# A two-layer decoder kernel on one core: forget rows from sigmoids, and the recurrent value projection by seven half-size products

## What is computed

```python
def hgrn2_mixer(u, w_in, lb, out_gain, w_out):
    q, fl, inp, g = split(u @ w_in)             # each 512 x 1024, 8 heads of 128
    log_f = logaddexp(log(lb), log1p(-lb) + log_sigmoid(fl))
    k = -expm1(log_f)
    # per head: b = cumsum(log_f); scores_ts = sum_d q_td k_sd exp(b_td - b_sd), s <= t
    # o = scores @ inp + (q exp(b)) @ state; o = rms_norm(o) * out_gain * silu(g)
    return o @ w_out
```

## Time and profile before

| | us |
|---|---|
| median of 3 runs (lowest, highest) | 2130.0 (2129.38, 2132.3) |
| the profiled execution, its time | 2130.18 |
| its span in the trace | 2126.7 |

### The profile page before, as it was taken

One profiled execution on the slowest core, in us unless ns is written; L12 is line 12 of the kernel. 1 busy time (PEld: TensorE's weight loads), 2 busy tenths in 40 slices (PEclk: granted clock), 3 DMA queues, 4 the chain that ended last, 5 costly groups with the idle time before them and its releaser, 6 DMA issues.

```text
span 2126.7 us, 20583 instructions
## 1 busy us (share of the span) xinstructions
PE 1986.8 (93%) x8264; PEld 1002.0 (47%) x8264; DVE 631.7 (30%) x1413; ACT 421.8 (20%) x833; POOL 268.4 (13%) x367
## 2 busy tenths in 40 slices
PE   8999999999999999999996998989898899979896
PEld 4588854444555544545543533424343434324333
DVE  2355542212888423242535101002020202001012
ACT  1033331116666211102311000100000010100002
POOL 3433100002767200001110000000000000000000
PEclk9999999999999999999998999999999999999998
DMA  9022230202110502411333699999999999999995
GB/s 265 3 60 60 91 138 0 80 10 88 60 40 25 212 16 99 121 40 40 109 130 158 272 427 428 427 427 427 427 428 428 427 427 427 427 428 425 428 425 201
DMA packets 100141, 486.59 MB, mean 229 GB/s; under 512 B 5855, under 2 KB 50234, under 8 KB 75984
## 3 DMA queue, kind: packets, MB, share of 16 engines
q1 hardware_dynamic: 97376, 480.79, 56.2%
q0 software_dynamic: 2384, 4.39, 0.7%
q10 hardware_dynamic: 288, 0.11, 0.0%
HBM read 483.13 MB, written 2.34 MB: 228 GB/s over the span
## 4 chain that ended last, share of the span: by engine, by line
PE 78%; DMA 12%; DVE 7%; ACT 2%; issue 1%; POOL 0%; POOLq 0%; ACTq 0%; DVEq 0%
PE bank L888 17%; PE bank L1370 13%; DMA arena<-in_w_up 12%; PE bank L1401 10%; PE bank L880 10%; PE bank L961 6%; PE bank L1321 3%; PE bank L1239 3%; PE bank L1347 2%; PE bank L985 2%; PE bank L1391 2%; PE bank L1125 1%; DVE arena L2033 1%; DVE arena L2032 1%; PE bank L870 1%
## 5 line engine op out<-in xcount | busy, mean ns | idle before, releaser
L1370 PE MATMUL bank<-arena 128*64 128x512 f32 x2048 | 466.3, 613 | 70.7 <-DMA arena<-in_w_up 70.6
L888 PE MATMUL bank<-arena 128*128 128x512 f32 x832 | 361.9, 595 | 5.1 <-issue 4.2
L1370 PEld LDWEIGHTS bank<-arena 128*64 128x64 f32 x2048 | 160.3, 141 | 373.7 <-issue 373.5
L880 PE MATMUL bank<-arena 128*128 128x512 f32 x672 | 295.3, 597 | 0.3
L888 PEld LDWEIGHTS bank<-arena 128*128 128x128 f32 x832 | 157.4, 191 | 198.8 <-issue 197.6
L1401 PE MATMUL bank<-arena 128*64 128x512 f32 x960 | 219.8, 617 | 0.0
L880 PEld LDWEIGHTS bank<-arena 128*128 128x128 f32 x672 | 127.2, 192 | 155.3 <-issue 155.1
L1456 ACT ACTIVATE arena<-bank 128x512 f32<-128x512 f32 (+3 forms) x134 | 72.7, 548 | 474.5 <-PE bank L888 193.2
L2382 DVE TENSOR_TENSOR arena<-arena,bank 128x512 f32<-128x512 f32 x64 | 42.0, 684 | 409.7 <-PE bank L1347 409.1
L2397 DVE TENSOR_TENSOR arena<-bank,arena 64x512 f32<-64x512 f32 x64 | 44.5, 695 | 365.5 <-ACT arena L1708 363.9
L1708 ACT ACTIVATE arena<-bank 64x512 f32<-64x512 f32 x64 | 37.6, 588 | 552.6 <-PE bank L1370 510.6
(11 more groups left out here) (308 smaller groups left out, 1800.0 us busy)
## 6 DMA issues: line engine op xcount, KB each, us to landing
arena<-in_w_gate SPq DMA_DIRECT2D x64, 2048.0 KB, 24.1
arena<-in_w_up SPq DMA_DIRECT2D x64, 2048.0 KB, 28.2
arena<-in_w_down SPq DMA_DIRECT2D x60, 2048.0 KB, 23.9
arena<-in_att_w_in SPq DMA_DIRECT2D x24, 512.0 KB, 7.3
arena<-in_rec_w_in SPq DMA_DIRECT2D x12, 1024.0 KB, 5.7
arena<-in_ple_w_gate SPq DMA_DIRECT2D x4, 2048.0 KB, 11.8
arena<-in_w_down SPq DMA_DIRECT2D x8, 1024.0 KB, 15.3
arena<-in_w_in SPq DMA_DIRECT2D x6, 1024.0 KB, 8.3
```

The lines of the kernel that those rows point to most:

```text
L880: mm = pe.matmul(bank[:, :], w[:, k, c:c + P], xT[:, k, :], start=(k == 0), stop=(k == KT - 1))
L888: mm = pe.matmul(bank[:, 0:n], xT[:, k, P * i:P * i + P], w[:, k, c:c + n], start=(k == 0), stop=(k == kt - 1))
L1370: mm = pe.matmul(banks[f][64 * part:64 * part + 64, :], xe[:, k, CAP * (e % 2):CAP * (e % 2) + CAP], w[:, kk, 512 * f:512 * f + 512], star ...
```

## The change

1. `i1` by seven products instead of eight (Strassen's scheme in Winograd's form). The 512 tokens are split into tiles (0, 1) and (2, 3), the 1024 channels and the 1024 columns into halves. Each of products 1 to 7 is done for two tiles, 4 matmuls of 512 columns each (`row_product`): 14 jobs, 56 matmuls. VectorE makes four sums of weights (`i1_weight_sum`, 128 x 2048 each, between the steps of `tail(0)`; the fourth goes to a buffer of its own), eight sums of tokens (128 x 512) after tile 3 is turned, and 14 additions of results, of which ScalarE did none before. ScalarE reverses tile 1 whole and half of tile 3, and drains four jobs instead of eight.
2. The forget rows from sigmoid(f) and sigmoid(-f), read straight from the bank; k and its reversed part by a scaled copy; log_f by one ln with scale and bias. VectorE keeps only the running sum.
3. In the head loop VectorE takes `forget_sum(h+2)` and levels 0 to 3 of `exponents(h+2)` ahead of the states of head h, level 4 before the mean, levels 5 and 6 after it. ScalarE takes `forget_rows(h+2)` ahead of the copy of the turned k, and `level_exps(h+2)` right after `chunk_exps(h+1)`. At the head start it copies both q rows before `level_exps(0)`.
4. Waits and loads named after `("i1", 3, 1)` are named after `("i1", 7, 1)`, the new last job.

```diff
+    def row_ending():
+        yield ("i1", 1, 0), "act"
+        yield from pre(1, 2)
+        yield ("i1", 1, 1), "act"
+        yield from row_part("i1", 2)
+        yield from pre(1, 3)
+        for p in (4, 6, 5, 3, 7):
+            yield from row_part("i1", p)
...
-        rec_slab("f1", 1, 4096, ("i1", 3, 1))
-        rec_slab("g1", 0, 6144, ("i1", 3, 1))
+        rec_slab("f1", 1, 4096, ("i1", 7, 1))
+        rec_slab("g1", 0, 6144, ("i1", 7, 1))
...
+            def row_product(name, x, w):
+                bank = job_bank(name)
+                for k in range(4):
+                    mm = pe.matmul(bank[:, :], x[:, k, :], w[:, k, :], start=(k == 0), stop=(k == 3))
+                mm.then_inc(filled, 1)
...
+            def input_rows():
+                wlo, whi = need_slab(pe, ("i1", 0)), need_slab(pe, ("i1", 1))
+                (s1, s2, s3, s4), (t1, t2, t4) = i1_sums, i1_weights
+                tile_done(("u", 1), 0)
+                row_product(("i1", 1, 0), UT[:, 0:4, 0:P], wlo[:, 0:4, :])
+                pre(1, 2, u_rows[0])
+                pe.wait_ge(tile_reversed, 1)
+                row_product(("i1", 1, 1), tile_1r[:, 0:4, :], wlo[:, 0:4, :])
+                row_product(("i1", 2, 0), UT[:, 4:8, 0:P], wlo[:, 4:8, :])
+                row_product(("i1", 2, 1), tile_1r[:, 4:8, :], wlo[:, 4:8, :])
+                pre(1, 3, u_rows[1])
+                pe.wait_ge(i1_summed, 4)
+                tile_done(("u", 1), 2)
+                row_product(("i1", 4, 0), UT[:, 4:8, 2 * P:3 * P], t4)
+                pe.wait_ge(tile_reversed, 2)
+                row_product(("i1", 4, 1), tile_3r, t4)
+                tile_done(("u", 1), 3)
+                for p, ready, x, w in ((6, 8, s2, t2), (5, 8, s1, t1), (3, 10, s4, whi[:, 4:8, :]), (7, 12, s3, whi[:, 0:4, :])):
+                    pe.wait_ge(i1_summed, ready)
+                    for t in range(2):
+                        row_product(("i1", p, t), x[:, :, P * t:P * t + P], w)
...
             def forget_in(h):
-                w = fwork[h % 2]
                 if h >= 2:
-                    act.wait_ge(f_dve, 3 * (h - 2) + 2)
+                    act.wait_ge(f_dve, h - 1)
+                if h >= 1:
+                    act.wait_ge(f_act, 2 * (h - 1) + 1)
                 act.wait_ge(filled, nth(("f1", h)))
                 bank = led.bank(("f1", h))
-                act.activation(w[0], bank[:, :], ACT.Identity)
-                act.activation(w[1], bank[:, :], ACT.Abs).then_inc(by_act, 1)
...
+                act.activation(logf1[h % 2], bank[:, :], ACT.Sigmoid)
+                act.activation(other1, bank[:, :], ACT.Sigmoid, scale=-1.0).then_inc(by_act, 1)
+
+            def forget_rows(h):
+                if h >= 2:
+                    act.wait_ge(filled, nth(("diag", h - 2)))
+                    act.wait_ge(decayed, 16 * (h - 2) + 16)
                 act.wait_ge(*drained(("f1", h)))
...
+                act.wait_ge(lb_dve, 2)
+                rest = lw[2][:, h:h + 1]
+                act.activation(k1[h % 2], other1, ACT.Identity, scale=rest)
+                act.activation(k1r[h % 2], other1.rearrange("p (c t) -> p c t", c=TT)[:, 1::2, ::-1], ACT.Identity, scale=rest
                                ).then_inc(f_act, 1)
...
+                act.activation(logf1[h % 2], logf1[h % 2], ACT.Ln, bias=lw[3][:, h:h + 1], scale=rest).then_inc(f_act, 1)
...
-            forget_in(0)
-            forget_softplus(0)
-            forget_in(1)
-            forget_floor(0)
-            copy(q1[0], ("q1", 0))
+            for h in range(2):
+                forget_in(h)
+                forget_rows(h)
+            for h in range(2):
+                copy(q1[h], ("q1", h))
             level_exps(0)
             chunk_exps(0)
...
+            level_exps(1)
             for h in range(RH):
-                if h + 1 < RH:
-                    level_exps(h + 1)
+                if h + 2 < RH:
+                    forget_rows(h + 2)
                 copy(kw1[:, :, :], ("kw", h), src=lambda b: b[:, 0:384].rearrange("p (c t) -> p c t", c=3))
...
                 if h + 1 < RH:
                     chunk_exps(h + 1)
+                if h + 2 < RH:
+                    level_exps(h + 2)
...
                 ple(2)
                 transposed(("h", layer), 3, 1, hT2, None)
                 turned(1)
+                if layer == 0:
+                    i1_weight_sum(1)
                 rows(2)
                 ple(3)
                 rows(3)
+                if layer == 0:
+                    i1_weight_sum(2)
                 turned(2)
+                if layer == 0:
+                    i1_weight_sum(3)
+                    i1_early_rows()
                 turned(3)
...
                 if h + 2 < RH:
-                    forget_log(h + 2)
+                    forget_sum(h + 2)
+                    exponents(h + 2, range(4))
                 head_states(h)
                 if h + 1 < RH:
                     chunk_exponents(h + 1)
...
                 if h + 2 < RH:
-                    forget_sum(h + 2)
+                    exponents(h + 2, range(4, 5))
                 head_mean_square(h)
                 if h + 2 < RH:
-                    exponents(h + 2)
+                    exponents(h + 2, range(5, LEVELS))
```

More of the change, by code:

```diff
@@ L179, in tail @@
                 yield from middle
+        if layer == 0:
+            yield from row_ending()
+            return
         yield from follow(0)
@@ L216, in psum_jobs @@
                 yield from joint("g0", m // 2)
-    yield from tail(0, lambda i: rows(("i1", i), "act", "act"))
+    yield from tail(0, None)
     for tag, h in FIRST_HEADS:
@@ L927, in tail @@
                         middle()
+                if layer == 0:
+                    follow()
+                    return
                 for i in range(TT):
@@ L1554, in _ @@
-            act.wait_ge(lb_dve, 2)
-            act.activation(lw[2], lw[1], ACT.Exp).then_inc(lb_act, 1)
-            act.wait_ge(lb_act, 1)
-            act.activation(lw[2], lw[2], ACT.Ln, bias=1.0).then_inc(lb_act, 1)
+            act.wait_ge(*drained(("u", 1, 1, 1)))
+            act.wait_ge(filled, nth(("gate", 0, 3, 1)))
+            act.activation(tile_1r, UT[:, :, P:2 * P][:, :, ::-1], ACT.Identity).then_inc(tile_reversed, 1)
+            for t in range(2):
+                copy(i1_first[t], ("i1", 1, t))
@@ L1559, in forget_in @@
+            act.wait_ge(*drained(("u", 1, 3, 1)))
+            act.activation(tile_3r, UT[:, 4:8, 3 * P:4 * P][:, :, ::-1], ACT.Identity).then_inc(tile_reversed, 1)
+            for t in range(2):
+                copy(i1[:, 2 + t, 0:512], ("i1", 4, t))
+            act.wait_ge(lb_dve, 1)
+            act.activation(lw[1], lw[0], ACT.Sigmoid).then_inc(lb_act, 1)
+            act.activation(lw[2], lw[0], ACT.Sigmoid, scale=-1.0).then_inc(lb_act, 1)
             def forget_in(h):
-                w = fwork[h % 2]
@@ new lines, in i1_early_rows, with i1_rows, block, token_sum @@
+            def i1_early_rows():
+                for t in range(2):
+                    dve.wait_ge(*drained(("i1", 1, t)))
+                    dve.wait_ge(filled, nth(("i1", 2, t)))
+                    dve.tensor_tensor(i1[:, t, 0:512], led.bank(("i1", 2, t))[:, :], i1_first[t], ALU.add).then_inc(by_dve, 1)
+            def i1_rows():
+                s1, s2, s3, s4 = i1_sums
+                def block(k, late, t):
+                    x = UT[:, 4 * k:4 * k + 4, P * (2 * late + t):P * (2 * late + t) + P]
+                    return x[:, :, ::-1] if t else x
+                def token_sum(dst, t, one, two, op):
+                    dve.tensor_tensor(dst[:, :, P * t:P * t + P], one, two, op).then_inc(i1_summed, 1)
+                def part(x, t):
+                    return x[:, :, P * t:P * t + P]
+                dve.wait_ge(*drained(("u", 1, 3, 1)))
+                for t in range(2):
+                    token_sum(s1, t, block(0, 1, t), block(1, 1, t), ALU.add)
+                for t in range(2):
+                    dve.wait_ge(i1_summed, 5 + t)
+                    token_sum(s2, t, part(s1, t), block(0, 0, t), ALU.subtract)
+                for t in range(2):
+                    dve.wait_ge(i1_summed, 7 + t)
+                    token_sum(s4, t, block(1, 0, t), part(s2, t), ALU.subtract)
+                for t in range(2):
+                    token_sum(s3, t, block(0, 0, t), block(0, 1, t), ALU.subtract)
+                def add(dst, p, t, more):
+                    dve.wait_ge(filled, nth(("i1", p, t)))
+                    return dve.tensor_tensor(dst, led.bank(("i1", p, t))[:, :], more, ALU.add)
+                lo, hi = slice(0, 512), slice(512, 1024)
+                first, second, fourth = i1_first, i1_second, i1_fourth
+                for t in range(2):
+                    add(second[t], 6, t, first[t]).then_inc(by_dve, 1)
+                for t in range(2):
+                    dve.wait_ge(*drained(("i1", 6, t)))
+                    dve.wait_ge(*drained(("i1", 4, t)))
```

(11 more changed lines are left out.)

118 lines of the change are left out of this document (45 added, 73 removed).

## The result

| | us |
|---|---|
| changed kernel, median of 4 runs (lowest, highest) | 2113.2 (2111.6, 2118.2) |
| kernel before, median of 4 runs beside it (lowest, highest) | 2130.6 (2129.4, 2132.3) |
| ratio of the two, with its 95% interval | 0.9913 [0.9894, 0.9931] |
| profiled execution of after: span | 2110.3 |

What follows compares the result with a forecast made beforehand. TensorE's matmuls were taken to bound the `i1` stage and, at 21.6 us per head plus waits and slow clock, the head loop. 2130.2 - 6.7 (products) - 16.6 (loop) = 2106.9, forecast 2107, range 2104.5 to 2114.

Steps and rivals of the forecast that it cites:

- A head therefore costs TensorE 21.6: Head loop: TensorE needs 21.6 us per head, so the other engines may save only its waits and the slow clock.
- Products, -6.7: Stage of `i1`: 16 fewer instructions save 6.87 us, less a wait of 0.15; the projections start at 480.5.
- Head start, 0: Start of the heads: `level_exps(0)` comes 2 us later behind both q copies, within five us of room, so no change.
- Loop, -16.6: Head loop: waits -13.6, slow clock -4.0, a new wait in head 0 +1.0; bounds -17.6 and -13.8.
- The slack of 2.3: Head loop: room of 2.3 us between VectorE's eight rows ending at 10.6 and its state copies from 12.9.
- VectorE near 17 a head: Head loop: VectorE loses four groups of instructions, 3.6 of 20.5 us per head, leaving 16.9.
- The norm: Head loop: VectorE's norm ends 21 us after the diagonal job, slack 4 before the next head's sixth level job.
- Clock: Head loop: slow stretches in three heads, 4.0 us together, go with the waits; clock 1.00.
- rival 1: Head loop: VectorE late at the states in every head; about 2122, by half of that 2113; chance 0.13.
- rival 4: Head loop: VectorE and GpSimd slow each other, slower than before; 2155 if all rows take 1.48; chance 0.04.
- Rivals 3 and 5: Products in `i1` don't pay, 2114, chance 0.06; sigmoids need as many table loads on ScalarE, 2108, within the forecast.
- rival 2: Head loop: waits gone but slow clock stays, following short waits too; 2111; chance 0.06.

Runs made afterwards that it cites:

- early exponentials: Changed kernel with level_exps(1) right behind chunk_exps(0), ahead of the gate copies: 2109.8 us in one execution, 2110.1 when timed.
- ln first: Changed kernel with level_exps(1) right behind chunk_exps(0) and, in the forget rows, the ln ahead of the two scaled copies for k: 2106.4 us.
- products alone: Kernel before with the seven products only, forget rows and both lists of the head loop as before: 2123.7 us, ratio 0.996.
- VectorE's old list: Changed kernel with ScalarE's new list kept, but VectorE's head-loop list in the order of before: 2137.9 us, ratio 1.0028.
- GpSimd nearly still: Changed kernel with GpSimd's level multiplies of heads 1 to 7 on one column, values of those heads left out: 2098.7 us in one execution.
- both old lists: Changed kernel with VectorE's and ScalarE's head-loop lists in the order of before, sigmoid rows and products kept: 2121.1 us, ratio 0.9948.
- six rows: Changed kernel with level_exps(1) right behind chunk_exps(0) and six exponent rows ahead of the states instead of eight: 2111.2 us, ratio 0.9902.

## Why the prediction was right, and where not

The time fell in the range, with help from its width. The forecast loop was 7.6 us too short, which by itself puts the sum at 2114.5, above the range; 0.7 less in the other stages and 2.4 us around the span instead of 3.5 brought it to 2112.7. And by its own signs the account failed: TensorE waits for the copies of the states in every head from 0 to 5, which the prediction had named as showing it wrong. Of its other limit, heads 22.5 apart, heads 1 to 5 stayed clear and heads 0 and 6 did not.

- **What bounds the kernel.** Right for the stage with `i1`, where the matmuls removed came back one to one. "A head therefore costs TensorE 21.6" was wrong by 0.8: the period less the waits shown still holds waiting time that counts as busy. It did no harm to the sum, since the heads stayed above it.
- **Products, -6.7.** Measured 480.30 for the end, forecast 480.5. Weight sums 2.28 each (2.3 estimated), token sums 4.91 for eight (5.2). Their cover held.
- **Head start, 0.** The first diagonal job stands 48.07 after the start, before 48.0. Right.
- **Loop, -16.6, bounds -17.6 and -13.8.** Measured -9.0: outside its own bounds. The miss of 7.6 is 3.9 in head 0 (25.4 for 21.5), 1.1 in heads 1 to 5 (21.8 for 21.6) and 2.3 in head 6 (24.9 for 22.6, before's 24.5 less its waits), with 0.3 of rounding.
- **The term that was mis-sized** is the eight rows ahead of the states. The price was 0.34 each, bound 0.57; they take 0.67 and start 0.5 to 0.9 apart (head 0: eight in 5.4 us). The scan ran 6.9 to 8.1 after the diagonal job, as forecast (to 7.9), but the rows ended at 13.5, not 10.6 or 11.8. The slack of 2.3 was overdrawn, and TensorE waits 0.7 in each of heads 1 to 5. In head 0 the running sum ended 10.1 after the diagonal job (9.6 forecast), the rows 15.5 (12.4 to 13.9), so the wait was 3.3 and not 0.5 to 2, and brought the clock down with it.
- **Why the rows of before misled.** The mean 0.57 of the earlier trace rows was of rows that lay mostly behind GpSimd's level multiplies. Before, two rows beside GpSimd's root on 4 columns, which leaves them at 0.42, and what GpSimd did then:

```profile
604.16 0.42 DVE L2032 TENSOR_TENSOR arena<-arena 128x256 f32<-128x256 f32 x1
604.50 0.41 DVE L2033 TENSOR_TENSOR arena<-arena 128x256 f32<-128x256 f32 x1
```

```profile
603.59 1.18 POOL L791 TENSOR_TENSOR small<-small 128x4 f32<-128x4 f32 x1 [0.17 <-DVE small L2081]
```

After, two rows, and two of the 21 level multiplies beside which the change puts them:

```profile
606.61 0.94 DVE L2126 TENSOR_TENSOR arena<-arena 128x256 f32<-128x256 f32 x1
607.48 0.67 DVE L2127 TENSOR_TENSOR arena<-arena 128x256 f32<-128x256 f32 x1
```

```profile
606.37 0.91 POOL L791 TENSOR_TENSOR arena<-arena 128x256 f32<-128x256 f32 x1
607.24 0.63 POOL L793 TENSOR_TENSOR arena<-arena 128x128 f32<-128x128 f32 x1
```

- **"VectorE near 17 a head".** Wrong: 20.6. The 3.6 us of removed instructions came back in the others: 1.8 in the rows (14 at 0.67 for 14 at 0.54) and 1.7 in the root's small steps (means 0.60, 0.98, 0.58 and 0.34 for 0.26, 0.16, 0.17 and 0.16), which now lie beside GpSimd's level multiplies and its multiply of a chunk (1.27).
- **The norm.** Its waits went, as forecast. It ends 23.0 after the diagonal job, not 21; its slack of 4 is 1.9.
- **Clock.** Forecast 1.00, measured 0.98: 0.93 in heads 0 and 6. Head 0's slow stretch follows its 3.3 us wait and goes with it (early exponentials). Head 6's follows waits of 0.4, 0.3 and 0.2, less than the 1.2 and 1.5 after which the earlier trace rows had shown 1.00. It is no matter of these waits alone: with the same ones head 6 ran at 1.00 in one kernel (early exponentials, its projection 7.13 us) and at 0.93 in another (ln first, 8.83), and with 1.2, 0.3, 0.2 and 0.2 at 1.00 before and at 0.94 with the products alone. What decides it is open. So 1.7 us of the loop's miss are a stretch that the edits don't control.
- **Rivals.** The place was that of rival 1, the states in every head, the cause that of rival 4, the two engines slowing each other. TensorE's waits for the states are 6.9 us, about half of rival 1's 12, and rival 1 at half price gave 2113, which is what was measured: the range was hit as much by that rival as by the forecast. To end above 2130, rival 4 needed 1.2 us per row; they took 0.67. Rivals 3 and 5 were wrong; rival 2 was right in head 6 alone, without its waits being gone.
- **Behind the loop** the stages last 447.3 and 946.2 (447.3 and 946.7 before): carried through one to one, as forecast.

## What to carry to other kernels

An engine's time freed by removing instructions is not free if the rest moves beside a neighbour that slows it: price a moved instruction by rows that lie beside what it will lie beside, not by the mean of its line. Where engines run on in-order lists, a wait reaches everything queued behind it, so check two lists that feed each other together (ScalarE's new order alone made the loop 20 us longer than both did). And when a wait moves from one place to another with the period unchanged to 0.01 us, look for what sets it elsewhere.

## What the runs showed of the hardware

- VectorE's instructions whose operands all lie in SBUF are slowed beside GpSimd's multiplies, small ones the most (128x4: 0.16 to 0.98 us); those that read a bank are not (0.526 and 0.524, 0.347 and 0.348). It goes both ways: GpSimd's 128x128 multiply beside VectorE's running sum took 1.44 us (604.32 in the changed kernel), others of its size there 0.45 to 0.70. And a row can be held up by several multiplies in a row: with VectorE's old list a row of 256 columns (L2137) began at 599.99 and took 2.47 us, ending 0.3 after the last of GpSimd's level multiplies (602.17); with GpSimd nearly still it takes 0.42.
- A single stall of VectorE, in the loop of one of the 14 traces and unexplained: L2217, 0.65 us in the changed kernel, took 6.03 in the profiled execution of the timed early exponentials. It made the states of head 6 late by 3.03 and head 6 last 28.1:

```profile
669.91 6.03 DVE L2217 TENSOR_SCALAR arena<-arena 64x512 f32<-64x512 f32 x1
```

- Executions differ by 6 us in a stage that no kernel here changed: in three of the profiled ones (VectorE's old list, both old lists, six rows) the clock was 0.95 between 100 and 200 us, where the others have 1.00. TensorE did fewer instructions there in the same busy time. First both old lists, then before:

```profile
100.00:200.00 100.00, 98.30 (x460) 77.14 (x459) 54.09 (x174) 32.57 (x89) 27.80 (x26) 0.95 0.26 64
```

```profile
100.00:200.00 100.00, 98.29 (x483) 78.88 (x482) 57.08 (x181) 32.72 (x90) 31.33 (x29) 1.00 0.26 64
```

What chooses between the two is open. It is why loops are compared here with loops. It also sits in the totals: six rows ahead, whose loop is 3.7 us shorter than the changed kernel's, was profiled in such an execution (2113.6).
